# The second memory's keys are split and turned in the o stage's input product, behind its first two units, and not at the beginning of the third FFN

## The reference

```python
def memory_cross_attention(h, m, w_q, w_kv, w_o, g_qn, g_kn):
    q = rms_norm_2((h @ w_q).reshape(B, S, XA_HEADS, XA_HEAD_DIM), g_qn)
    kv = m @ w_kv
    k = rms_norm_2(kv[..., :XA_WIDTH].reshape(B, M, XA_HEADS, XA_HEAD_DIM), g_kn)
    v = kv[..., XA_WIDTH:].reshape(B, M, XA_HEADS, XA_HEAD_DIM)
    logits = jnp.einsum('bshd,bmhd->bhsm', q, k).astype(jnp.float32) / np.sqrt(XA_HEAD_DIM)
    ...
for layer in range(DEPTH_2):          # layer 1 is the odd one
    x = x + mixer(rms_norm_2(x, g_mix[layer]))
    x = x + memory_cross_attention(rms_norm_2(x, g_xa[layer]), m, ...)
    x = x + swiglu_2(rms_norm_2(x, g_ffn[layer]), ...)
```

## Time and profile before

| | |
|---|---|
| median of 3 runs | 1213.09 us (1212.29 to 1213.5) |
| the profiled execution, its own time | 1212.66 us |
| its span in the trace | 1210.8 us |
| PE busy | 1202.2 us |
| DVE busy, ACT busy | 774.0 us, 691.9 us |
| DMA queue of SP, of ACT (share of 16 engines) | 56.8%, 5.1% |
| granted clock of PE, mean | 1.0 |

### The profile page before, as it was taken

One profiled execution on the slowest core, in us unless ns is written; L12 is line 12 of the kernel. 1 busy time (PEld: TensorE's weight loads), 2 busy tenths in 40 slices (PEclk: granted clock), 3 DMA queues, 4 the chain that ended last, 5 costly groups with the idle time before them and its releaser, 6 DMA issues.

```text
span 1210.8 us, 17122 instructions
## 1 busy us (share of the span) xinstructions
PE 1202.2 (99%) x5662; PEld 989.1 (82%) x5662; DVE 774.0 (64%) x1089; ACT 691.9 (57%) x1012; POOL 68.8 (6%) x119
## 2 busy tenths in 40 slices
PE   9999999999999999999999999999999999999998
PEld 7888888877788888888888788788888887888887
DVE  6665555788686566567678765665556667665554
ACT  7555545566655555557676576555555546755543
POOL 0520000000000000000220110000000000000000
PEclk9999999999999999999999999999999999999999
DMA  9977754554565999754654517976655554776771
GB/s 338 248 221 230 215 176 151 158 162 143 165 201 178 238 245 256 218 158 158 206 168 165 174 63 228 244 229 202 201 161 167 164 161 149 212 220 200 221 225 44
DMA packets 208386, 232.01 MB, mean 192 GB/s; under 512 B 56081, under 2 KB 148369, under 8 KB 208337
## 3 DMA queue, kind: packets, MB, share of 16 engines
q1 hardware_dynamic: 163792, 214.61, 56.8%
q10 hardware_dynamic: 42752, 11.02, 5.1%
q0 software_dynamic: 1792, 5.75, 1.9%
HBM read 219.78 MB, written 1.05 MB: 182 GB/s over the span
## 4 chain that ended last, share of the span: by engine, by line
PE 95%; DVE 2%; DMA 1%; ACT 1%; issue 0%; ACTq 0%; SPq 0%; DVEq 0%
PE bank L1969 29%; PE bank L1971 29%; PE bank L1970 29%; PE bank L2028 2%; PE bank L2196 1%; DMA sb_probs<-sb_probs 1%; DVE sb_wl L1318 1%; PE bank L2183 1%; PE bank L2212 1%; PE bank L2181 0%; DMA sb_raw<-w_out 0%; ACT sb_probs L1235 0%; ACT sb_wh L733 0%; PE bank L2058 0%; PE bank L2500 0%
## 5 line engine op out<-in xcount | busy, mean ns | idle before, releaser
L1969 PE MATMUL bank<-sb_wh,sb_aTh 128*128 128x512 f32 (+1 forms) x1124 | 436.6, 388 | 0.5 <-issue 0.3
L1971 PE MATMUL bank<-sb_wh,sb_aTl 128*128 128x512 f32 (+1 forms) x1124 | 431.1, 384 | 0.0
L1970 PE MATMUL bank<-sb_wl,sb_aTh 128*128 128x512 f32 (+1 forms) x1124 | 430.8, 383 | 0.0
L1318 DVE TENSOR_TENSOR sb_wl<-sb_raw,sb_wh 128x1024 fp32r<-128x1024 f32 x269 | 325.6, 1222 | 104.5 <-ACT sb_wh L733 100.1
L733 ACT ACTIVATE sb_wh<-sb_raw 128x1024 fp32r<-128x1024 f32 (+1 forms) x275 | 286.3, 1048 | 114.0 <-PE bank L1971 38.7
L1969 PEld LDWEIGHTS bank<-sb_wh,sb_aTh 128*128 128x128 f32 x1124 | 211.3, 188 | 43.0 <-issue 2.4
L1971 PEld LDWEIGHTS bank<-sb_wh,sb_aTl 128*128 128x128 f32 x1124 | 211.2, 188 | 42.1
L1970 PEld LDWEIGHTS bank<-sb_wl,sb_aTh 128*128 128x128 f32 x1124 | 211.5, 188 | 39.6
L1318 DVE TENSOR_TENSOR sb_wl<-sb_z,sb_wh 128x1024 fp32r<-128x1024 f32 x132 | 158.7, 1221 | 37.9 <-ACT sb_wh L733 37.8
L733 ACT ACTIVATE sb_wh<-sb_z 128x1024 fp32r<-128x1024 f32 x132 | 137.2, 1057 | 59.5 <-PE bank L1971 42.4
L1969 PE MATMUL bank<-sb_wh,sb_hTh 128*128 128x512 f32 x320 | 125.2, 391 | 1.1 <-DVE sb_hTl L1400 1.0
(11 more groups left out here) (218 smaller groups left out, 918.6 us busy)
## 6 DMA issues: line engine op xcount, KB each, us to landing
sb_raw<-w_in SPq DMA_DIRECT2D x80, 256.0 KB, 3.0
sb_z<-ffn_w_down SPq DMA_DIRECT2D x64, 256.0 KB, 5.0
sb_z<-w_down SPq DMA_DIRECT2D x64, 256.0 KB, 3.8
sb_raw<-w_gate SPq DMA_DIRECT2D x54, 256.0 KB, 3.4
sb_raw<-w_up SPq DMA_DIRECT2D x54, 256.0 KB, 4.2
sb_raw<-ffn_w_gate SPq DMA_DIRECT2D x51, 256.0 KB, 3.7
sb_raw<-ffn_w_up SPq DMA_DIRECT2D x51, 256.0 KB, 4.4
sb_raw<-e_w_in SPq DMA_DIRECT2D x40, 256.0 KB, 3.0
```

What stands on the lines that cost most here:

```text
L1318: dve.tensor_tensor(wl[:, u % NSPLIT, :], raws[SLOT[u]], wh[:, u % NSPLIT, :].bitcast(F32), ALU.subtract).then_inc(low_done, 1)
L1969: pe.matmul(dst, lh, w_hi, start=start, stop=False)
L1970: pe.matmul(dst, lh, w_lo, start=False, stop=False)
L1971: return pe.matmul(dst, ll, w_hi, start=False, stop=stop)
```

## The change

On ACT, the two copies and the DMA transpose of the second memory's keys leave the beginning of FFN 2, where the split of one unit stood between them; that split goes back to its place in `body(0)`. They come into the o stage: the copies behind the split of unit 5, the transpose's issue behind that of unit 6. Nothing else is different.

```diff
@@ ffn(f), ACT @@
                 ht_step(1, hTh[:, :, :])
-                if f == 2:
-                    km_split(1, 4)
-                    split(u + 4)
-                    km_turn(1)
-                body(0, False, begun=1 if f in (0, 2) else 0)
+                body(0, False, begun=1 if f == 0 else 0)
@@ o stage, ACT @@
             xt_high(6, 1)
             split(u0)
             token_ssq(6, x)
-            splits(u0 + 1, 3)
+            split(u0 + 1)
+            km_split(1, 4)
+            split(u0 + 2)
+            km_turn(1)
+            split(u0 + 3)
             rstd_known(6)
 
             evac(u0 + 4, 0, 6, z[:, :, 0, :], odd_evac_a)
```

## The result

The kernel with the change takes **1216.23 us** (median of 7 runs, 1214.82 to 1216.91), the kernel before, run beside it, 1212.49 us (7 runs, 1211.34 to 1213.92): ratio 1.0031, 95% interval 1.0022 to 1.0041. That is 3.7 us slower, where I had forecast +0.9 and a range up to 1215.6 us.

What follows compares the result with a forecast made beforehand. PE was taken to bound the kernel, 95% of the chain of waits. -1.6 us in FFN 2 and +2.5 us in the o stage gave +0.9 on 1212.66, so 1213.6 us, range 1211.3 to 1215.6.

Steps and rivals of the forecast that it cites:

- Should start some 3.7 us earlier: FFN 2: without the key copies and issue, the hidden values' DMA turn starts about 3.7 us sooner.
- fits: FFN 2: even a hidden turn as slow as the slowest seen reaches PE in time, with 0.2 us to spare.
- A gain of 1.6 us: FFN 2: the time saved, middle of the 1.44 to 1.74 us it took beyond FFN 1 and FFN 3.
- The chain in the o stage: Copies, unit 6's split, turn issue, unit 7's split 3.0 us late, DVE's subtraction and evacuation, then PE's pool product.
- Makes PE wait 2.5 us: O stage, pool product: DVE's evacuation, 0.5 us early before, comes 3.0 us late, so PE waits 2.5 us.
- I take 2.83: O stage: the key turn's issue holds ACT for 2.83 us as in FFN 2, rather than 1.34.
- a load of SP under way: O stage: reason for choosing 2.83 us: the turn meets unit 8's load, already issued by SP.
- The slower rival: O stage: unit 8's load holds up turn and ACT; issue 6.3 us, PE waits 6.0, 1217.1 us; chance 0.10.
- A short issue: O stage: issue takes 1.34 us like the first memory's, PE waits 1.0, total 1212.1 us; chance 0.25.
- the issue hardly holds ACT: O stage: only copies delay unit 7's split, 1.0 us; PE waits 0.5, total 1211.6 us; chance 0.08, shared with no wait.
- the gain does not come: FFN 2: hidden turn stays late for another reason, with full o stage cost, 1215.2 us; chance 0.05.
- What moves behind it: After the o stage copies: later subtractions, loads of units 9 and 10, pool maps and key join; put down at nothing.

Runs made afterwards that it cites:

- late: The change, with key copies and turn moved behind ACT's copy of the pooled values for the pool maps: 1211.52 us, ratio 0.9998.
- quiet: The change, with key copies between FFN 2's last splits and the turn ahead of the o stage: 1211.46 us, ratio 0.9998.
- turn far from loads: The change, with copies at FFN 2's end and the whole turn issued behind both parts of `xt_high`, away from SP's loads: 1212.88 us, ratio 1.0003.
- added turn: Kernel before, keeping FFN 2's key split and turn, with a second split and turn at the change's o stage place: 1216.41 us, ratio 1.0037.
- idle by copies: Kernel before, turn left in FFN 2, with four more key-plane copies on ACT ahead of unit 7's split: 1215.98 us, ratio 1.0028.
- halves: The change, with eight blocks of the turn issued at its place and eight behind the evacuation: 1212.74 us, ratio 1.0002.
- copies alone: The change, with the turn's issue moved behind the evacuation and the two copies left ahead of unit 7's split: 1211.98 us, ratio 0.9997.

## Why the prediction was wrong

- **The removal in FFN 2.** "Should start some 3.7 us earlier" and "fits": right, 8.83 us and no wait. **"A gain of 1.6 us" failed in its size:** the mean over three profiles is 1.1. I took the FFN's length from one execution, in which the key turn's issue was long (2.83 us, against 2.54 and 1.98 in the other two) and the hidden turn went out and landed late. That is 0.5 us.
- **The chain in the o stage.** Right link by link: copies 2.0 us, unit 7's split behind the issue, DVE's two instructions, PE. "Makes PE wait 2.5 us" was 3.09, because **"I take 2.83" failed:** the issue took 3.46 us here and 2.8 to 3.9 for whole turns anywhere in this stretch. "A longer issue than 2.83 is not shown by any row, nor excluded" was the honest half of that sentence. My reason, a load of SP under way, is not borne out. 0.6 us.
- **What the sum left out.** The sum ended at PE's wait. **A term was missing, put at nothing without a reason: 1.7 us of matmuls at half clock behind the wait.** This is the largest of the three and the one without which the time would have been inside the range: the one run at full clock took 1214.82 us.
- **The sum with measured sizes:** -1.1 + 3.1 + 1.7 = +3.7 us; the medians differ by 1216.23 - 1212.49 = 3.7. That the sum agrees to a tenth is luck. Worked out from each run without the keys in FFN 2, as what it costs from FFN 2 to FFN 3 in its trace less what it costs by medians, the gain is 0.3 us (late and quiet) to 1.5 (turn far from loads).
- **The rivals.** The slower rival named the right place and the wrong price: it needed an issue of over 4.3 us, and none was. A short issue (1.34 us) did not come. That the issue hardly holds ACT fell clearly: unit 7's split waited 2.51 us for it. That the gain does not come fell too: FFN 2 took 155.54 us.
- **What moves behind it** (later loads, pool maps, the join): put down at nothing, and it was next to nothing here; 3.09 + 1.7 leaves 0.1 of the 4.9 us. The run with the turn far from SP's loads shows that such a delay can come back through a load.

## What to carry to other kernels

Price a wait of TensorE by its length and by what follows it: when a change opens idle time longer than any already in the trace (here 1.3 us was the longest wait of PE before), ask what the granted clock does behind it, and break the wait up or fill it. Take the price of a wait that hangs on a DMA's landing from several executions. And put a DMA issue on a compute engine's queue behind what the bounding engine waits for: the same turn behind the pool's evacuation cost PE nothing.

## What the runs showed of the hardware

- **The clock fell behind the longest waits of PE, in most runs.** Matmul starts 3.45, 3.32 and 2.74 us apart (added turn, the change, idle by copies) were followed by about 3.4 us at half clock, in profiles; 2.09, 1.16 and 0.90 us (turn far from loads, halves, copies alone) at the same place were not, nor were 1.44 us in FFN 2 and 1.89 there in the run idle by copies. Not in every run: one of seven with the change, one of eight with the copies and two of five with the added turn kept the mean at 1.0. The Trainium skill, "TensorE: Matmul & The Clock Gate", Part 1, says that the array's clock goes back to half when PE has been idle; the trace agrees, with the 1.7 us that it cost here.
- **The issue of a DMA transpose is no constant.** A turn of 16 blocks held ACT for 1.34 to 1.39 us at the first memory, 1.92 to 2.99 us in FFN 2, and 2.77 to 3.94 us between FFN 2's end and the pool maps; 8 blocks for 1.25 to 1.84.
